# A hybrid decoder layer on eight cores: one load planned later, position tables made in another stage, and the last tile's sums, products and table load rearranged

## The reference

```
h = h + 0.5 * swiglu(rmsnorm(h)) with weights ffn1 (1024 -> 2816 -> 1024)
u = rmsnorm(h);  z = u @ w_in
o_mla = causal attention, 8 heads, low-rank q and kv, rotary part of 32 columns by position
o_gla = chunked gated linear attention, 4 heads
o_x   = cross-attention, 4 heads, into 256 memory tokens (rmsnorm(mem) @ x_w_kv)
h = h + (sigmoid(gz0) * o_mla @ Wa + sigmoid(gz1) * o_gla @ Wb + sigmoid(gz2) * o_x @ Wc) @ w_out
h = h + 0.5 * swiglu(rmsnorm(h)) with weights ffn2
return rmsnorm(h) * final_norm
```

## Time and profile before

| | us |
|---|---|
| median of 3 runs | 1656.39 (1656.03 to 1881.89) |
| the profiled execution | 1660.75 |
| its span, slowest core (core 7) | 1659.7 |
| spans of the 8 cores | 1650.2 to 1659.7 |
| TensorE busy | 1616.8 (97%) |
| VectorE busy | 873.4 (53%) |
| ScalarE busy | 744.1 (45%) |
| GpSimd busy | 120.2 (7%) |

### The profile page before, as it was taken

The page is one execution under the profiler, slowest core; times in us unless marked ns, Lnnn a source line. Parts: engine busy times, 40 slices in busy tenths (PEclk is TensorE's granted clock), DMA queues, the critical chain, the costliest instruction groups (busy, mean ns, idle before and its releaser), DMA issues.

```text
span 1659.7 us, 23972 instructions; the slowest of 8 cores (1650.2 to 1659.7 us)
## 1 busy us (share of the span) xinstructions
PE 1616.8 (97%) x7691; PEld 741.1 (45%) x7691; DVE 873.4 (53%) x1501; ACT 744.1 (45%) x1195; POOL 120.2 (7%) x227
## 2 busy tenths in 40 slices
PE   7999999999999989999999999999999999999996
PEld 2445444434444434444434444444444444444443
DVE  5663442535766475664554445477344445533345
ACT  4213011156863256873266874247586623311114
POOL 0101011100000000000000000000100000011000
PEclk9999999999999999999999999999999999999998
DMA  8779998976575556586778878587324354523213
GB/s 205 112 124 126 146 122 113 143 167 168 128 155 161 171 122 135 94 195 182 235 204 199 182 168 208 185 276 245 104 94 128 120 160 163 173 70 101 77 38 102
DMA packets 80393, 249.15 MB, mean 150 GB/s; under 512 B 9424, under 2 KB 13776, under 8 KB 79824
## 3 DMA queue, kind: packets, MB, share of 16 engines
q0 software_dynamic: 28720, 107.43, 36.8%
q1 hardware_dynamic: 51552, 140.18, 26.6%
HBM read 282.89 MB, written 54.00 MB: 203 GB/s over the span
## 4 chain that ended last, share of the span: by engine, by line
PE 89%; DMA 5%; DVE 2%; ACT 2%; issue 1%; SPq 0%; DVEq 0%; ACTq 0%; POOLq 0%
PE ps_all L560 89%; DMA spill<-hS 1%; DMA ring<-f1g 1%; DMA hS<-x 1%; DMA ring<-wb 1%; ACT L586 1%; DMA rstd<-ma 1%; ACT ma L586 0%; DVE hS L598 0%; ACT mb L586 0%; DVE B L598 0%; ACT fa L586 0%; DVE aF L593 0%; DVE ma L593 0%; ACT B L609 0%
## 5 line engine op out<-in xcount | busy, mean ns | idle before, releaser
L560 PE MATMUL ps_all<-ntm,ring 128*128 128x512 bf16 x2224 | 534.0, 380 | 0.1
L560 PE MATMUL ps_all<-B,ring 128*128 128x512 bf16 x2016 | 453.4, 379 | 0.7 <-DMA ring<-f1g 0.3
L560 PEld LDWEIGHTS ps_all<-ntm,ring 128*128 128x128 bf16 x2224 | 217.1, 98 | 256.8 <-issue 8.7
L560 PE MATMUL ps_all<-aF,ring 128*128 128x512 bf16 (+1 forms) x1264 | 301.8, 378 | 4.3 <-ACT B L609 2.1
L560 PEld LDWEIGHTS ps_all<-B,ring 128*128 128x128 bf16 x2016 | 196.6, 98 | 234.5 <-issue 3.9
L586 ACT ACTIVATE fa<-ps_all 128x512 f32<-128x512 f32 x170 | 101.2, 597 | 397.8 <-PE ps_all L560 389.1
L598 DVE SCALAR_TENSOR_TENSOR hS<-ps_all,hS 128x512 f32<-128x512 f32 (+1 forms) x256 | 170.7, 672 | 105.7 <-PE ps_all L560 103.9
L593 DVE TENSOR_TENSOR aF<-fa,ps_all 128x512 bf16<-128x512 f32 x151 | 103.0, 685 | 224.8 <-PE ps_all L560 216.0
L586 ACT ACTIVATE mb<-ps_all 128x512 bf16<-128x512 f32 (+1 forms) x304 | 165.0, 573 | 74.7 <-PE ps_all L560 71.4
L560 PEld LDWEIGHTS ps_all<-aF,ring 128*128 128x128 bf16 x1264 | 124.3, 99 | 147.7 <-issue 12.2
L586 ACT ACTIVATE ma<-ps_all,hv 128x512 f32<-128x512 f32 x104 | 71.1, 687 | 165.8 <-PE ps_all L560 159.3
(11 more groups left out here) (136 smaller groups left out, 1179.7 us busy)
## 6 DMA issues: line engine op xcount, KB each, us to landing
ring<-wb SPq DMA_DIRECT2D x112, 512.0 KB, 4.5
ring<-f1g POOLq DMA_DIRECT2D x44, 512.0 KB, 9.7
ring<-f2bg POOLq DMA_DIRECT2D x44, 512.0 KB, 3.6
wb<-wm POOLq DMA_DIRECT2D x28, 512.0 KB, 15.2
ma<-spill SPq DMA_DIRECT2D x48, 256.0 KB, 5.5
ring<-wb SPq DMA_DIRECT2D x48, 256.0 KB, 3.4
ring<-f2g POOLq DMA_DIRECT2D x22, 512.0 KB, 7.4
f2bg<-ring SPq DMA_DIRECT2D x22, 512.0 KB, 7.2
```

The lines of the kernel that those rows point to most:

```text
L560: i = e.matmul(_ap(o), lhsT=_ap(l), rhs=_ap(r), start=st, stop=sp)
```

## The change

It has four parts.

1. The load of tile 3's x gets a slack of 10 in the plan (line 1316).
2. All four tables are made in the first channel mixer, after blocks 2, 3, 4 and 5. Tables 2 and 3 are written into a temporary instead of `CS` and stored in DRAM (`cs_later`), 128 KB each. In place of the old calls `load_table(2)` and `load_table(3)` read them into `CS[0]` and `CS[1]`, which are the same tiles, with a slack of 4.
3. In `ending` the two banks of the sums are of kind "n" instead of "f"; and in the first half the last of the four matmuls of each down product is an operation of its own, so that the planner can place the other three earlier.
4. In `ending` a logarithm of one column is written down ahead of the down products. It depends on the last activation of the tile.

```diff
@@ -474,6 +474,7 @@
     wm_d = din("wm", [NMB, 128, 2048])
     xw_d = din("xw", [4, 128, 2048])
     out_d = nc.dram_tensor("outT", [NT, 128, 8 * TT], F32, kind="ExternalOutput").ap()
+    cs_d = nc.dram_tensor("cs_later", [2, 64, TT], F32).ap()
     wb_d = nc.dram_tensor("wb", [NMB, 128, 2048], BF16).ap()
     sp_d = nc.dram_tensor("spill", [NT, 128, 8 * TT], F32).ap()
     f2bg_d = nc.dram_tensor("f2bg", [ND, 128, 2048], BF16).ap()
@@ -645,12 +646,12 @@
 
 
 
-    def load_x(t, slot, after=None):
+    def load_x(t, slot, after=None, slack=0.0):
         ops = []
         for c in range(0, 8, 2):
             op = f.dma("sp", R(hslot[slot][c], hAP[slot][:, c:c + 2, :]),
                        x_d[t][:, c * TT:(c + 2) * TT].rearrange("p (c n) -> p c n", c=2),
-                       outs=[hslot[slot][c + 1]], nbytes=524288, after=after)
+                       outs=[hslot[slot][c + 1]], nbytes=524288, after=after, slack=slack)
             ops.append(op)
         return ops
 
@@ -714,9 +715,17 @@
         ts(m, a, -math.pi, TWO_PI, ALU.is_lt, ALU.mult)
         tt(a, a, m, ALU.add)
         ts(a, a, 3.1415925, -3.1415925, ALU.min, ALU.max)
-        actf(CS[t], a, AF.Sin)
-        ts(CS[t][32:64, :], CS[t][32:64, :], vecs[96:128, V_SG:V_SG + 1], None, ALU.mult)
+        table = CS[t] if t < 2 else m_[q, :]
+        actf(table, a, AF.Sin)
+        ts(table[32:64, :], table[32:64, :], vecs[96:128, V_SG:V_SG + 1], None, ALU.mult)
+        if t >= 2:
+            f.dma("sp", csT[t - 2], table, nbytes=131072)
         M2.put(p_, a_, k_, m_)
+
+    csT = [T(cs_d[i], f"cs_later{i}") for i in range(2)]
+
+    def load_table(t):
+        f.dma("sp", CS[t], csT[t - 2], nbytes=131072, slack=4.0)
 
     def mean_square(srcs, dim, n, banks, narrow):
         p = bank(banks)
@@ -1284,7 +1293,7 @@
         if j == 1:
             M2.put(*[r for _, r in raws])
             late_constants()
-        if j in (2, 3):
+        if j in (2, 3, 4, 5):
             f.base = LATER // 2
             rope_tables(j - 2)
             f.base = 0
@@ -1313,7 +1322,7 @@
             take_over(NTB[0] + NTB[1], hslot[2])
             return
         take_over(NTB[2], aT[2])
-        load_x(3, 1)
+        load_x(3, 1, slack=10.0)
 
     ffn(f1_d, [nB[0], nB[1], nB[2]], (0, 1, 2), "f", True, lambda i, c: sums[i].take(hslot[i][c]), side1,
         by_tile=(1, 0, 2), opening=OPENING, closed=close1, acts=[aT[0], aT[2], aT[1]])
@@ -1341,9 +1350,9 @@
         return make
 
     mixer_tile(0, nM[0], lambda: norm_from_dram(1, V_MIX, nM[1]), quiet, norm_here(0, 0), hslot[0])
-    rope_tables(2)
+    load_table(2)
     mixer_tile(1, nM[1], lambda: norm_from_dram(2, V_MIX, nM[2]), quiet, lambda r: keep_rstd(1, r, M2))
-    rope_tables(3)
+    load_table(3)
 
     f.mark("ffn2a")
 
@@ -1390,13 +1399,18 @@
             for c in range(8):
                 take_over([hh[h][c]], [hslot[i][c]])
         ps_ = []
+        early = M2.get()
+        actf(early[:, 0:1], eps_c, AF.Ln, extra_ins=(act[len(w[0]) - 1],))
+        M2.put(early)
         for h in range(2):
             cols = slice(h * 256, (h + 1) * 256)
-            p = bank("f")
+            p = bank("n")
             ps_.append(p)
             for c in range(8):
                 py = bank("f")
-                mm([(py[:, cols], w[c][j], act[j][:, cols], j == 0, j == len(w[c]) - 1) for j in range(len(w[c]))])
+                m = len(w[c])
+                for js in (range(m - 1), (m - 1,)) if h == 0 else (range(m),):
+                    mm([(py[:, cols], w[c][j], act[j][:, cols], j == 0, j == m - 1) for j in js])
                 stt(hh[h][c], py[:, cols], 0.5, hh[h][c], ALU.mult, ALU.add)
                 sq = M1.get()
                 actf(sq[:, 0:256], hh[h][c], AF.Square, scale=D ** -0.5)
```

## The result

The changed kernel takes a median of 1638.71 us (1637.26 to 1719.23, 6 runs); the kernel before, run beside it, 1657.64 us (1656.03 to 1881.89, 6 runs). The ratio is 0.9886, 95% interval 0.9871 to 0.9902: 18.9 us less (1.1%), within the 2% band. The prediction was 1640.0 (1633 to 1651). Ratios here, and the intervals, leave disturbed runs out; the medians of the raw runs don't, so they are not divided.

What follows compares the result with a forecast made beforehand. TensorE's matmuls bound the kernel, leaving its idle time and clock losses to gain. 5 + 5.5 + 4.2 + 4.2 - 1.5 - 1 = 16.4 us off the median 1656.4 gives 1640, range 1633 to 1651.

Steps and rivals of the forecast that it cites:

- What bounds the kernel: Whole kernel: matmuls fill 1616.8 of 1659.7 us; only TensorE's 42.9 us idle and time below full clock can be gained.
- Tile 3's x: At 355.7 to 359.6 us: slack removes a 3.9 us wait and 1.35 us clock loss; 5 us gain, ends 0 and 5.2.
- Tables 2 and 3: Projections of tiles 1 and 2: moving table work off VectorE ends waits for copies; gains of 5.5 and 4.2 us.
- The same tables in the first channel mixer, and the late tokens: First channel mixer: tables delay the memory tokens' loads, kv weights hold ring buffers; 1.5 us loss, bounds 0 and 18.1.
- The last tile: From 1635 us: sum banks, split last step and early log load shorten the end; 4.2 us gain, full worth 4.9.
- A new plan: Everything behind 100 us: the planner's order changes and waits come or go; 1 us loss, ends -2 and 10.
- The profiled execution before: Profiled run took 1660.8 us, 4.4 above the median 1656.4; forecast 1644.4 against its own time, 1640.0 against the median.
- Rival 1: Projections: the copies themselves gate; half of the tables' 9.7 us is lost, 1645; chance 0.18.
- Rival 2: New waits elsewhere, tile 3's norm beside tile 2's squares and tile 0's projections; 10 us of waits, 1650; chance 0.10.
- Rival 3: First channel mixer's second group, 161 to 190 us: late memory tokens delay down blocks; 1660, net +4; chance 0.07.
- Rival 5: Low-priority tables slide into tile 0's projections; the 9.7 us not gained, 1.5 us not paid, 1648; chance 0.03.
- Rival 4: Last tile: log table load delays the first squares by 1.6 us; tile gives 2.2 instead of 4.2, 1642; chance 0.05.

Runs made afterwards that it cites:

- x alone: Kernel before with only the slack of 10 on tile 3's x load: ratio 1.0075 (1.0056 to 1.0095), slower by 12 us.
- the work done once more: Whole change plus the work of tables 2 and 3 repeated at the old places, read by nobody: ratio 1.0083 to the kernel before, slower by 14 us.
- two neighbours of the same change, the two kernels with the early start: Kernel before with slack 10 on tile 3's x only, ratio 1.0075; whole change with unread table work repeated at the old places, 1.0083.

## Why the prediction was right, step by step

- **What bounds the kernel.** Right: idle and clock losses carry the whole difference, 12.0 + 10.5 us of span. But 5.1 of the 10.5 are the stretches at 0.81 on cores 4 to 7, which belong to the execution that was profiled before and not to the change.
- **Tile 3's x** (5 us, ends 0 and 5.2). The wait and its slow slice are gone, as said. But the size holds only against the old order. In the order that the tables' edit makes, the wait for x is 7.1 to 7.7 us, with 3 to 4 us of clock and ring waits behind it; there the slack of 10 is worth 14 to 16 us. Without the tables' edit it costs 12, and a slack of 15 gains 9.8.
- **Tables 2 and 3** (5.5 + 4.2). Both projections are fully busy, with the tables' edit alone as with the whole. But the worth is not confirmed. With the loss in the first mixer taken off, the terms net 5.5 + 4.2 - 1.5 = 8.2 us; the edit alone gave 2.3 us (0.7 to 4.2), and beside x with slack 15 and the last tile about 1 us, as other waits came up. And the tables' work is not the whole cause of these waits: with x alone and with the work done once more, it stands at both projections, and the waits for copies are 0.4 to 0.6 and 1.6 to 2.1 us in all, against 6.8 to 7.3. So the order in which the copies and the products stand sets these waits too, and neither a term nor a rival of mine had that.
- **The same tables in the first channel mixer, and the late tokens** (1.5, bounds 0 and 18.1). Four Sin before 200 us and kv at 175 us came as written; the tokens' loads came at 120 to 140 us, in part earlier than the 130 to 145 I gave. The mechanism is the one I named: while the kv weights hold ring buffers, one down block lands late. Between the f1d loads issued at 143.4 and 160.7 us stands one other, where the kernel before issued three from 145.2 to 155.1. That the kv weights' buffers are what held them back fits this and was not tested alone. Only the size was off: 3.7 us on the slowest core, more than double the term. Three cores have 2.3 us of it, a fourth 1.3.
- **The last tile** (4.2 of a full worth of 4.9): 4.98 us in the trace of the whole change, 4.0 by the ratio of the part alone (interval 1.0 to 7.0). The idle before the adds fell from 6.1 to 1.4 us, below the 2 that I wrote, and the last scaling ends 7.4 us after the last add, where I had 6.5: 0.9 of it is a wait for ScalarE's powers.
- **A new plan** (1, ends -2 and 10). This is the step that held only by luck. The changed kernel has one new wait of 4 us, at 735 us, and not 1; and two neighbours of the same change show that the term reaches some +17 (for x alone the sum without this term is 5 us of gain; measured were 12 of loss, so 17). My upper end of 10 was too low, and the range of 1633 to 1651 would have missed both of them. That the sum came within 1.3 us of the median is in part luck too: the tables' net term was too large by some 6 us as far as it was measured, and x inside the whole change too small by 9 or more.
- **The profiled execution before.** I took its own time 4.4 us above the median and gave a figure against each. Against its own time I had 1644.4, and the profiled execution after took 1638.18; against the median I had 1640.0, and it is 1638.71. The second is the better measure, since 5.1 us of that execution were the stretches at 0.81.
- **The rivals.** Rival 1, copies gate with the tables gone: rejected, 22.00 of 22 us busy. Rival 2, new waits elsewhere: not in the changed kernel beyond some 8 us, but it is the outcome of x alone, with its mechanism, in another place than I gave. Rival 3, late tokens: it came, in its place and with its down block, at a fifth of its price. Rival 5, tables slide: rejected by the Sin at 139.5 and 151.8 us.
- **Rival 4, the log load in front of the squares.** Rejected. The logarithm starts 0.01 us behind the end of the 1.28 us load, at 1620.81, and the first square 0.11 us later, at 1620.92, as 1620.11 + 0.42 = 1620.53 is the end of the first add: 0.4 us of delay, with 1.1 us gained when the load is alone. The Trainium skill (ScalarE: Activation LUTs, What ACT_TABLE_LOAD costs) budgets a drain behind the load, 2.66 us for each switch; no trace here shows one, in either place, so the measurement decides for 1.28.

**What stays open.** Why the planner starts the filler at 1008 us with one slack and at 1098 us with another was not isolated. That the early start and the late holes go together is shown: in 1320 to 1440 us the two kernels with the early start idle 13 to 17 us on every core, and all twelve other traces at most 1.1 us. That the one makes the other is argued. Open too is what removing the tables' work is worth by itself.

## What to carry to other kernels

When a program's order is made by a planner, price the waits at their places, and then give the new order a term of its own as wide as the whole expected gain: here single edits of the change came out at +12, -2 and -4 us, and together at -21; with another slack the first was -10, and then the parts added up. Look at the covers that lie far behind the edit (what fills the last stage, and is it still there?) before believing a single part's result, and try two or three values of a slack, since 10 and 15 differed by 22 us. Work moved into a busy stage with idle VectorE is cheap but not free: name which loads and buffers it delays. When a wait's named releaser goes on working after the wait has ended, look for a DMA that landed at that moment. And before a term is taken for a cause, look for a run in which the cause stands and the wait does not.

## What the runs showed of the hardware

TensorE's granted clock fell after short waits too: after an idle of 2.28 us the next 5 us ran at 0.72, and 170 to 172 us within them at 0.50; after 2.46 us the stretch of the wait had 0.66, and 736 to 738 us within it 0.50. So a part of each ran at the 1.2 GHz level. The stretches at 0.81 of the kernel before are another thing: no wait stands within the 15 us before the one at 881 to 889 us, TensorE is busy throughout, and cores 4 to 7 have it together while cores 0 to 3 read 1.00. What brings it on no run here shows. It cost 5.1 us in one execution, which is about what that execution stood above its median (4.4 us).

One and the same load of a down block took 14.1 us to land on three cores of the changed kernel and 13.1 us on a fourth, and that microsecond is the difference between waits of 2.3 and 1.3 us.
